# Two-layer hybrid trunk: output and second feed-forward products with tokens on partitions

## The chip, the cores and the metric

The kernel runs on one core of one Trainium2 chip. The metric is the device time of one execution in microseconds (us). Three executions of the kernel before took 1070.94, 1072.71 and 1075.98 us; the median is 1072.71 us.

## The reference

The program computes two layers of a trunk on 256 tokens of width 1024, in float32. Only the ends of the two halves of a layer matter here:

```
for l in range(2):
    u = rms_norm(x, pre_mix_norm_w[l])
    proj = u @ w_in[l]
    ...                                  # gated delta rule, latent attention, gates
    h = gates[:, :, 0] * y_a + gates[:, :, 1] * y_b
    x = x + rms_norm(h @ w_out[l], post_mix_norm_w[l])      # "out", 1024 x 1024
    u = rms_norm(x, pre_ffn_norm_w[l])
    f = square(relu(u @ w_ff1[l])) @ w_ff2[l]               # "ff1" 1024 x 4096, "ff2" 4096 x 1024
    x = x + rms_norm(f, post_ffn_norm_w[l])
```

`rms_norm(y, w)` is `y * rsqrt(mean(y*y over the 1024 features) + 1e-6) * w`.

## The kernel before

All activations lie with features on partitions: `xT` is 128 partitions x 8 chunks of features x 256 tokens. A float32 product is made of three fp32r products: the operand and the weight are each split into a high part (rounded) and a low part (the rest), and high x high, high x low and low x high are added up in PSUM.

The weights stream in pieces of 128x1024 float32 (512 KB), 152 a layer, through a ring of four places: SyncE issues the DMA into `raw`, ScalarE rounds it into `whi` (L973), VectorE subtracts into `wlo` (L1296), TensorE uses it in 24 matmuls (L559 to L561, in `chunk_products`) and raises `steps_done`, which frees the place. TensorE waits for `lo_ready`, which VectorE raises after each `wlo`.

The work is a list of jobs (`jobs_of_a_layer`), each with its pieces, and `schedule` writes one order, `ORDER`, that every engine walks through, doing its own part of each entry. Between the entries ScalarE and VectorE do the weight splits; `splits_wanted` (L488) says up to which piece each has to have split before its part of an entry, normally four pieces past the job's last one. So the place of a split in an engine's queue is fixed by the order in the program.

A job of "out" or "ff2" makes 256 features of all 256 tokens in one PSUM bank of `dense`: per 128x128 block of weights (stationary) three matmuls of 128x256 (the activations move). There are four such jobs of 2 pieces ("out") and four of 8 pieces ("ff2") a layer. After each, ScalarE squares the bank (L1095), VectorE multiplies it with the norm's weight into `yT` (L1591), and GpSimd adds up squares (L1697). After the fourth, `ysum` (L948) sums squares over features on TensorE by matmuls with a matrix of ones (L955), which leaves the row sum on every partition; ScalarE makes the inverse root by a logarithm and an exponential (L984, L986); VectorE multiplies `yT` with it and adds it to `xT` in pairs of chunks, two of the four adds done by GpSimd (`post`, L1612 and L1729). Then ScalarE rounds `xT` times the next norm's weight (`fuh` at L1037, or `xh` at L1003 for the next layer), VectorE takes the rest (`ful` at L1632, `xl` at L1303), and the next product starts, chunk by chunk: its first piece covers chunks 0 to 3, the second chunks 4 to 7. "ff1" comes after "out", the latent projection "lat" of the next layer after "ff2", the output DMAs after the last "ff2".

Of the kernel before, what the change touches and what calls it, by code (L numbers as in the profile page):

```python
# [19 lines left out]
ALU = mybir.AluOpType  # L20
# [3 lines left out]
P = 128  # L24
# [36 lines left out]
def jobs_of_a_layer():  # L61
# [3 lines left out]
    for kind, numbers, pieces in (("lat", range(3), 2), ("k", range(1), 2), ("z", range(1), 2), ("k", range(1, 4), 2),  # L65
# [4 lines left out]
                                  ("out", range(4), 2), ("ff1", range(16), 2), ("ff2", range(4), 8)):  # L70
# [8 lines left out]
EVAC_BY_ACT = {"v", "q", "k", "uq", "kn", "vt", "z", "gate"}  # L79
NJOB = len(JOBS)  # L80
NACT_EVAC = sum(k in EVAC_BY_ACT for k, _, _ in JOBS)
NDVE_EVAC = NJOB - NACT_EVAC
# [17 lines left out]
def evacs_through(j):  # L100

    mine = JOBS[j][0] in EVAC_BY_ACT
    return mine, sum((k in EVAC_BY_ACT) == mine for k, _, _ in JOBS[:j + 1])


def schedule():
# [129 lines left out]
    for i in range(4):  # L236
        job("ff2", i)
        if i in (1, 2):
            o.append(("yadd", 1 + i))
    o += [("ysum", 1), ("post", 1)]  # L240
# [7 lines left out]
def build(nc, x_in, pos_in, w_in, prm_in, cst_in, out):  # L248
    with ExitStack() as ctx:
# [32 lines left out]
        rs = keep("rs", [P, 4])  # L282
        bias_cols = keep("bias_cols", [P, 3])
# [68 lines left out]
        yT = ph("yT", [P, KD, S], 120)  # L352
# [47 lines left out]

        def S_(name):
            return ctx.enter_context(nc.semaphore(name))
# [18 lines left out]
        x_by_pool, x_by_dve, y_add = (signal("x_by_pool", 4), signal("x_by_dve", 4), signal("y_add", 4))  # L421
# [32 lines left out]
        h_hi, h_lo, y_sq, y_mm = (signal("h_hi", 4), signal("h_lo", 4), signal("y_sq", 8), signal("y_mm", 2))  # L454
        y_r, y_scaled, f_sq = (signal("y_r", 4), signal("y_scaled", 8), signal("f_sq", 16))
# [4 lines left out]
        def due(l, s, n):  # L460

            return l * rises_per_layer[s.name] + n

# [46 lines left out]
        def _(sp):  # L510
# [10 lines left out]
            for c in range(4):  # L521
                pair = slice(2 * c, 2 * c + 2)
                x_pair = x_by_pool if c % 2 else x_by_dve
                sp.wait_ge(x_pair, due(DEPTH, x_pair, 1 + c // 2))
# [5 lines left out]
        def _(pe):  # L530
# [3 lines left out]
            def banks_free(l, j):  # L534

                if j >= 3:
                    by_act, n = evacs_through(j - 3)
# [26 lines left out]
            def half(l, j):  # L564
# [7 lines left out]
                chunk_products(dense[j % 3], n, 0, 4, 256, uh, ul, True, False, KD, need).then_inc(steps_done, 1)  # L572

            def job(l, j):
                kind, i, pieces = JOBS[j]
                bank = dense[j % 3]
# [17 lines left out]
                elif kind in ("ya", "yb", "out"):  # L594
                    a_, b_ = {"ya": (oh, ol), "yb": (ah, al), "out": (hh, hl)}[kind]
# [3 lines left out]
                    def need(k):  # L599
                        if kind == "ya" and i == 0:  # L600
                            pe.wait_ge(on_lo, due(l, on_lo, k // 2 + 1))
                        if kind == "out" and i == 0:
                            pe.wait_ge(h_lo, due(l, h_lo, k // 2 + 1))
# [43 lines left out]
                elif kind == "ff2":  # L647
                    for h_, n in enumerate(pieces):
                        piece(l, n)
                        if i == 0:  # L650
                            pe.wait_ge(f_lo, due(l, f_lo, 2 * h_ + 2))
                        r = chunk_products(bank, n, 4 * h_, 4, 256, fh, fl, h_ == 0, h_ == 7, KF)
                        r.then_inc(steps_done, 1)
# [294 lines left out]
            def ysum(l, w):  # L948

                pe.wait_ge(y_add, due(l, y_add, 2 * w + 2))  # L950
                for n in range(2):
                    if n:
                        pe.wait_ge(y_sq, due(l, y_sq, 4 * w + 4))
                    for e in range(2):
                        r = mm(side[1][:, 0:S], ones, sq[n][:, e * S:(e + 1) * S], start=(n == 0 and e == 0),  # L955
                               stop=(n == 1 and e == 1))
                r.then_inc(y_mm, 1)
# [3 lines left out]
                      sc=sc, tr=tr, pv=pv, ysum=ysum, qrope=qrope)  # L961
# [7 lines left out]
        def _(act):  # L969
# [18 lines left out]
            def x_there(l, w, c):  # L988

                if l == 0 and w == 0:  # L990
                    act.wait_ge(s_x[c], 16)
                else:
                    x_pair = x_by_pool if c % 2 else x_by_dve
                    act.wait_ge(x_pair, due(l, x_pair, 1 + 2 * w + c // 2))

            def xsplit(l, part):

                for e in (range(2), range(2, KD))[part]:
                    if e % 2 == 0:
                        x_there(l, 0, e // 2)  # L1000
# [5 lines left out]
            def sq_(l, n):  # L1006
                w, c = divmod(n, 4)
                pair = slice(2 * c, 2 * c + 2)
                x_there(l, w, c)
# [21 lines left out]
            def fsplit_x(l, _):  # L1031

                for c in range(KD):
                    x_pair = x_by_pool if c // 2 % 2 else x_by_dve
                    if c % 2 == 0:
                        act.wait_ge(x_pair, due(l, x_pair, 3 + c // 4))
# [17 lines left out]
            def job(l, j):  # L1054
                kind, i, _ = JOBS[j]
                bank = dense[j % 3]
                if kind not in EVAC_BY_ACT and kind not in ("lat", "out", "ff2"):
                    return
                act.wait_ge(steps_done, products_done(l, j))
# [31 lines left out]
                elif kind in ("out", "ff2"):  # L1091
# [790 lines left out]
```

## Time and profile before

| | |
|---|---|
| median of three executions | 1072.71 us |
| span of the profiled execution, first to last instruction | 1064.2 us |
| TensorE busy (matmul) | 1010.9 us, 95% |
| VectorE busy | 732.4 us, 69% |
| ScalarE busy | 557.7 us, 52% |
| GpSimd busy | 137.9 us, 13% |
| mean granted TensorE clock | 0.985 |

The profiled execution has no time of its own beside its span. The span runs from the first to the last instruction; the median of the executions is 8.5 us above it. In the views, a time is the start in us from the span's start, and PEclk is the share of the full clock (2.4 GHz) that TensorE was granted, so 0.50 is 1.2 GHz.

### The profile page before, as it was taken

Reading aid. Unit: us, or ns where it says so; the run is one execution under the profiler, and the core shown is the slowest. Engines: PE = TensorE matmul, PEld = TensorE weight load, DVE = VectorE, ACT = ScalarE, POOL = GpSimd, SP = SyncE. Lnnn points to the kernel's source line nnn. Section 1 sums busy time; section 2 is a strip of 40 time slices with the busy share of each in tenths; the row PEclk is TensorE's granted clock in tenths of the full one; section 3 lists DMA queues with packets and bytes.
Section 4 is the critical chain, followed back from the end, with each engine's and each line's share of the span. In section 5 each row is a group of like instructions: output and inputs, shape, how many; then the busy total and the mean of one; then the engine's idle time right before and its main releaser. Section 6 shows DMA issues by size and latency. Waiting matters only on the chain.

```text
span 1064.2 us, 24113 instructions
## 1 busy us (share of the span) xinstructions
PE 1010.9 (95%) x10552; PEld 987.3 (93%) x10552; DVE 732.4 (69%) x982; ACT 557.7 (52%) x786; POOL 137.9 (13%) x109
## 2 busy tenths in 40 slices
PE   5899899999999899999978999999999989999996
PEld 5899889899999899999978998998999979999995
DVE  6886648698566698745388766677875777886453
ACT  6576365755444554443356753767454445444441
POOL 6201000230000322200010000014000013221001
PEclk9999999999999899999989999999999999999998
DMA  7344424334556176666534443334356544766661
GB/s 252 135 141 158 124 82 130 118 106 149 188 180 197 65 224 192 200 196 195 160 119 135 143 142 121 115 106 121 117 166 189 166 153 145 213 197 199 193 185 40
DMA packets 45608, 163.85 MB, mean 154 GB/s; under 512 B 5184, under 2 KB 5440, under 8 KB 45504
## 3 DMA queue, kind: packets, MB, share of 16 engines
q1 hardware_dynamic: 44928, 161.50, 48.2%
q8 instruction: 83, 1.36, 0.5%
q10 hardware_dynamic: 576, 0.82, 0.2%
q14 instruction: 21, 0.17, 0.0%
HBM read 161.25 MB, written 1.05 MB: 153 GB/s over the span
## 4 chain that ended last, share of the span: by engine, by line
PE 91%; DVE 5%; issue 2%; ACT 2%; DMA 1%; POOL 0%; POOLq 0%; SPq 0%; ACTq 0%; DVEq 0%
PE dense L559 25%; PE dense L560 25%; PE dense L561 24%; DVE wlo L1296 1%; PE sides L945 1%; PE sides L799 1%; PE sides L919 1%; PE sides L920 1%; PE sides L791 1%; DVE utmp L1332 1%; PE sides L955 1%; PE sides L759 1%; PE sides L769 1%; PE sides L895 1%; PE sides L718 1%
## 5 line engine op out<-in xcount | busy, mean ns | idle before, releaser
L1296 DVE TENSOR_TENSOR wlo<-raw,whi 128x1024 fp32r<-128x1024 f32 (+1 forms) x304 | 397.9, 1318 | 195.8 <-ACT whi L973 195.5
L973 ACT ACTIVATE whi<-raw 128x1024 fp32r<-128x1024 f32 (+1 forms) x304 | 315.6, 1047 | 225.7 <-PE dense L561 222.0
L559 PE MATMUL dense<-uh,whi 128*128 128x256 f32 x768 | 223.3, 291 | 5.3 <-DVE wlo L1296 5.3
L560 PE MATMUL dense<-ul,whi 128*128 128x256 f32 x768 | 216.3, 282 | 2.6 <-issue 2.6
L561 PE MATMUL dense<-uh,wlo 128*128 128x256 f32 x768 | 216.3, 282 | 0.0
L559 PEld LDWEIGHTS dense<-uh,whi 128*128 128x128 f32 x768 | 147.2, 192 | 7.8 <-DVE wlo L1296 5.7
L559 PE MATMUL dense<-fuh,whi 128*128 128x256 f32 x512 | 144.3, 282 | 9.9 <-DVE ful L1632 9.6
L561 PEld LDWEIGHTS dense<-uh,wlo 128*128 128x128 f32 x768 | 147.2, 192 | 1.6 <-issue 1.6
L560 PEld LDWEIGHTS dense<-ul,whi 128*128 128x128 f32 x768 | 146.7, 191 | 1.5 <-issue 1.3
L560 PE MATMUL dense<-ful,whi 128*128 128x256 f32 x512 | 143.5, 280 | 0.0
L561 PE MATMUL dense<-fuh,wlo 128*128 128x256 f32 x512 | 143.5, 280 | 0.0
L559 PE MATMUL dense<-fh,whi 128*128 128x256 f32 x512 | 141.3, 276 | 0.0
L560 PE MATMUL dense<-fl,whi 128*128 128x256 f32 x512 | 141.3, 276 | 0.0
L561 PE MATMUL dense<-fh,wlo 128*128 128x256 f32 x512 | 141.3, 276 | 0.0
L559 PEld LDWEIGHTS dense<-fuh,whi 128*128 128x128 f32 x512 | 98.3, 192 | 11.1 <-issue 10.3
L560 PEld LDWEIGHTS dense<-ful,whi 128*128 128x128 f32 x512 | 98.2, 192 | 0.1
L561 PEld LDWEIGHTS dense<-fuh,wlo 128*128 128x128 f32 x512 | 98.1, 192 | 0.0
L560 PEld LDWEIGHTS dense<-fl,whi 128*128 128x128 f32 x512 | 96.1, 188 | 0.0
L559 PEld LDWEIGHTS dense<-fh,whi 128*128 128x128 f32 x512 | 96.1, 188 | 0.0
L561 PEld LDWEIGHTS dense<-fh,wlo 128*128 128x128 f32 x512 | 96.1, 188 | 0.0
L1727 POOL TENSOR_TENSOR fr<-fr 128x512 f32<-128x512 f32 x32 | 46.5, 1453 | 119.3 <-DVE fr L1604 119.3
L1697 POOL TENSOR_TENSOR sq<-sq,sq 128x512 f32<-128x512 f32 x8 | 10.4, 1296 | 353.0 <-ACT sq L1095 353.0
(289 smaller groups left out, 1923.2 us busy)
## 6 DMA issues: line engine op xcount, KB each, us to landing
raw<-weights SPq DMA_DIRECT2D x304, 512.0 KB, 3.7
xT<-x_t SPq DMA_DIRECT2D x4, 256.0 KB, 5.7
out_t<-xT SPq DMA_DIRECT2D x4, 256.0 KB, 2.3
cst<-consts ACTq DMA_DIRECT2D x1, 512.0 KB, 6.5
prm_all<-params ACTq DMA_DIRECT2D x1, 150.0 KB, 4.0
pos_i<-pos ACTq DMA_DIRECT2D x1, 128.0 KB, 5.5
cst<-consts ACTq DMA_DIRECT2D x1, 6.0 KB, 5.8
```

The lines of the kernel that those rows point to most:

```text
L559: mm(o_, h_[:, ws], ahi[:, k0 + k, :], start=is_first, stop=False, skip_group_check=True)
L560: mm(o_, h_[:, ws], alo[:, k0 + k, :], start=False, stop=False, skip_group_check=True)
L561: x_ = mm(o_, l_[:, ws], ahi[:, k0 + k, :], start=False, stop=is_last, skip_group_check=True)
L718: r = mm(side[KS_BANK[i // 2]][:, c:c + 1], k_squares[i][:, e * S + t * P:e * S + (t + 1) * P], ones[:, 0:1], start=True, stop=True)
L759: r = mm(side[KK_BANK[n]][:, e * P:(e + 1) * P], kT[:, h, ts_], kT[:, h, ts_], start=True, stop=True)
L769: r = mm(side[QK_BANK[n]][:, e * P:(e + 1) * P], kT[:, h, ts_], qT[:, h, ts_], start=True, stop=True)
L791: r = mm(side[e][rows, 16 * g:16 * (g + 1)], LT[rows, g, e, rows], evens(Xq[rows, e, g, :], SIZES[lv]), start=True, stop=True)
L799: r = mm(side[e][rows, 16 * g:16 * (g + 1)], XTq[rows, e, g, :], PBq[rows, e, g, 0:16], start=True, stop=True)
L895: mm(side[2 + i % 2][:], ones, sq[i % 2][:], start=True, stop=True).then_inc(on_mm, 1)
L973: return A(o_, i_, ACT.Copy)
L1296: TT(wlo[s][:, 0:w], raw[s][:, 0:w], f32(whi[s][:, 0:w]), ALU.subtract).then_inc(lo_ready, 1)
L1727: G(fr[i % 4][:], fr[i % 4][:], fr[i % 4][:], ALU.mult).then_inc(f_sq, 1)
```

## The change

- "out" and "ff2" are each two jobs of 512 features (4 and 16 pieces). The activations of 128 tokens are now the stationary operand and 512 columns of weights move, so a matmul is 128x512 and there are half as many. The result has tokens on partitions, in four banks of `side`: `y_bank(f, t)` for feature half f and token half t.
- In the second job of each, the last two pieces (`HELD`) are first used for tokens 0 to 127 (`y_mm` is raised), then for tokens 128 to 255 (`steps_done`, twice).
- The sum of squares is a row sum, made by ScalarE's accumulator while it squares (`y_square`): after the first job for half the features, whose mean VectorE prepares (`ysq`), after the second for the rest. The matmuls with ones, GpSimd's additions, `yT` and the products with the inverse root as 128x256 tiles go.
- The inverse root is a 128x1 column. ScalarE scales the rows of tokens 0 to 127 and half of those of tokens 128 to 255 into `yr`, VectorE the other half. TensorE turns `yr` back by 16 transposes of 128x128 (`post`).
- VectorE multiplies each turned chunk with the norm's weight and adds it to `xT` in one instruction, chunk by chunk, in turn with the low parts. GpSimd does nothing there.
- The splits of the third and fourth piece past "out" move behind `post` and `fsplit_x`, to a new entry `("ahead", 0)` of the order.
- TensorE waits, at the end of the first job of each, for its own products before it raises `y_mm`.

```diff
-                                  ("out", range(4), 2), ("ff1", range(16), 2), ("ff2", range(4), 8)):
+                                  ("out", range(2), 4), ("ff1", range(16), 2), ("ff2", range(2), 16)):
...
-    for i in range(4):
-        job("out", i)
-        if i in (1, 2):
-            o.append(("yadd", i - 1))
-    o += [("ysum", 0), ("post", 0), ("fsplit_x", 0)]
+    job("out", 0)
+    o.append(("ysq", 0))
+    job("out", 1)
+    o += [("post", 0), ("fsplit_x", 0), ("ahead", 0)]
...
+        def turn_bank(w, c):
+
+            return [side[4], dense[2 if w else (BANK[JOB["ff1", 0]] + 2) % 3], side[0], side[2]][c]
...
             if what == "job":
-                ahead = 2 if n == NJOB - 1 else RING
+                ahead = RING - HELD if JOBS[n][:2] in (("out", 1), ("ff2", 1)) else RING
                 return min(l * NPIECE + JOBS[n][2][-1] + ahead, DEPTH * NPIECE)
...
+            if what == "ahead":
+                return l * NPIECE + JOBS[JOB["out", 1]][2][-1] + RING
...
+            def by_token(l, kind, f, pieces):
+
+                w = kind == "ff2"
+                a_, b_, low_ready = (fh, fl, f_lo) if w else (hh, hl, h_lo)
+
+                def token_products(p, n, t):
+                    bank = y_bank(f, t)
+                    for e in range(2):
+                        k = 2 * p + e
+                        ws = slice(e * 512, (e + 1) * 512)
+                        ts_ = slice(t * P, (t + 1) * P)
+                        last = k == 2 * len(pieces) - 1
+                        mm(bank[:], a_[:, k, ts_], whi[n % RING][:, ws], start=(k == 0), stop=False)
+                        mm(bank[:], a_[:, k, ts_], wlo[n % RING][:, ws], start=False, stop=False)
+                        r = mm(bank[:], b_[:, k, ts_], whi[n % RING][:, ws], start=False, stop=last)
+                    return r
+
+                held = HELD if f else 0
+                for p, n in enumerate(pieces[:len(pieces) - held]):
+                    piece(l, n)
+                    if f == 0:
+                        pe.wait_ge(low_ready, due(l, low_ready, p + 1))
+                    token_products(p, n, 0)
+                    r = token_products(p, n, 1)
+                    r.then_inc(steps_done, 1)
+                if f == 0:
+                    pe.wait_ge(steps_done, l * NSTEP + steps_through(JOB[kind, 0], job=True) + RING)
+                    pe.sem_inc(y_mm, 1)
+                    return
+                late = list(enumerate(pieces))[len(pieces) - held:]
+                for p, n in late:
+                    piece(l, n)
+                    r = token_products(p, n, 0)
+                r.then_inc(y_mm, 1)
+                for p, n in late:
+                    r = token_products(p, n, 1)
+                    r.then_inc(steps_done, 1)
...
             def post(l, w):
-                act.wait_ge(y_mm, due(l, y_mm, w + 1))
-                rsqrt(l, y_r, w, rn[0][:, 0:S], side[1][:, 0:S], 1.0 / D, 0.0)
+
+                def scaled(t, a_, b_):
+                    f = a_ // 512
+                    A(yr[:, t, a_:b_], y_bank(f, t)[:, a_ - 512 * f:b_ - 512 * f], ACT.Identity,
+                      scale=yss[:, 4 + t:5 + t]).then_inc(y_by_act, 1)
...
+                def add(e):
+                    dve.wait_ge(y_turned, due(l, y_turned, 4 * w + e // 2 + 1))
+                    STT(xT[:, e, :], turn_bank(w, e // 2)[:, e % 2 * S:(e % 2 + 1) * S], col(l, (POST_FFN if w else POST_MIX) + e),
+                        xT[:, e, :], ALU.mult, ALU.add).then_inc(x_new, 1)
...
+                dve.wait_ge(y_r, due(l, y_r, 4 * w + 4))
+                for c in range(2):
+                    part = slice(256 * c, 256 * (c + 1))
+                    TS(yr[:, 1, part], y_bank(0, 1)[:, part], yss[:, 5:6], None, ALU.mult).then_inc(y_by_dve, 1)
                 add(0)
-                times_norm(1)
-                low(0)
-                times_norm(2)
-                add(2)
-                low(1)
-                times_norm(3)
-                low(2)
-                low(3)
+                for e in range(KD):
+                    if e + 1 < KD:
+                        add(e + 1)
+                    low(e)
```

ScalarE between "out" and "ff1", in the kernel before: `sq` is the square of the last job's bank, `rn_68` the inverse root, `whi` a weight split.

```order
L973 ACTIVATE whi_55<-raw_51 128x1024 [waits steps_done,loaded1]
L973 ACTIVATE whi_56<-raw_52 128x1024 [waits steps_done,loaded2]
L1095 ACTIVATE sq_67<-dense 128x512 [waits y_add,steps_done]
L984 ACTIVATE rn_68<-sides,bias_cols 128x256 [waits y_mm]
L986 ACTIVATE rn_68<-rn_68 128x256 [waits y_r]
L1037 ACTIVATE fuh<-xT,prm_all 128x256 [waits x_by_dve]
```

And in the changed kernel, from the first square of the last job to the first splits of "ff1" (`yss` are columns of sums and roots).

```order
L1144 ACTIVATE sq_66,yss<-sides 128x512 [waits y_mm]
L1038 ACTIVATE yss<-yss 128x1 [waits y_mean,y_ss]
L1040 ACTIVATE yss<-yss 128x1 [waits y_r]
L1312 ACTIVATE yr<-sides,yss 128x512 [waits y_r]
L1312 ACTIVATE yr<-sides,yss 128x512
L1144 ACTIVATE sq_67,yss<-sides 128x512 [waits steps_done]
L1038 ACTIVATE yss<-yss 128x1 [waits y_mean,y_ss]
L1040 ACTIVATE yss<-yss 128x1 [waits y_r]
L1312 ACTIVATE yr<-sides,yss 128x256 [waits y_r]
L1312 ACTIVATE yr<-sides,yss 128x256
L1087 ACTIVATE fuh<-xT,prm_all 128x256 [waits x_new] x8
L1027 ACTIVATE whi_55<-raw_51 128x1024 [waits steps_done,loaded1]
```

The rounding of the second piece of "ff1" into `whi_55` stood ahead of the last square and now stands behind all eight `fuh`.

VectorE in the same place, in the kernel before, from the last weight splits of "out".

```order
L1296 TENSOR_TENSOR wlo_59<-raw_51,whi_55 128x1024 [waits hi_ready]
L1296 TENSOR_TENSOR wlo_60<-raw_52,whi_56 128x1024 [waits hi_ready]
L1591 TENSOR_SCALAR yT<-dense,prm_all 128x256 [waits y_sq,steps_done]
L1591 TENSOR_SCALAR yT<-dense,prm_all 128x256
L1618 TENSOR_TENSOR yT<-yT,rn_68 128x512 [waits dve_evac,y_r]
L1623 TENSOR_TENSOR xT<-xT,yT 128x512 [waits y_scaled]
L1618 TENSOR_TENSOR yT<-yT,rn_68 128x512
L1632 SCALAR_TENSOR_TENSOR ful<-xT,prm_all,fuh 128x256 [waits fu_hi,x_by_dve]
```

And in the changed kernel; the middle chunks, alike but for the bank, are left out by the break between the two pieces.

```order
L1701 TENSOR_SCALAR yr<-sides,yss 128x256 [waits y_r]
L1701 TENSOR_SCALAR yr<-sides,yss 128x256
L1686 SCALAR_TENSOR_TENSOR xT<-sides,prm_all,xT 128x256 [waits y_turned] x2
L1693 SCALAR_TENSOR_TENSOR ful<-xT,prm_all,fuh 128x256 [waits fu_hi]
L1686 SCALAR_TENSOR_TENSOR xT<-dense,prm_all,xT 128x256 [waits y_turned]
```

```order
L1686 SCALAR_TENSOR_TENSOR xT<-sides,prm_all,xT 128x256 [waits y_turned]
L1693 SCALAR_TENSOR_TENSOR ful<-xT,prm_all,fuh 128x256 [waits fu_hi] x2
L1369 TENSOR_TENSOR wlo_59<-raw_51,whi_55 128x1024 [waits hi_ready]
L1369 TENSOR_TENSOR wlo_60<-raw_52,whi_56 128x1024 [waits hi_ready]
L1369 TENSOR_TENSOR wlo_61<-raw_53,whi_57 128x1024 [waits hi_ready]
```

The subtraction into `wlo_59`, for which TensorE waits before the second piece of "ff1", stood ahead of the norm and now stands behind the last `ful`.

## Rows read from the trace of the kernel before

**Rows 1.** The page's busy time, share of the span and instructions, by engine.
```profile
PE 1010.9 (95%) x10552; PEld 987.3 (93%) x10552; DVE 732.4 (69%) x982; ACT 557.7 (52%) x786; POOL 137.9 (13%) x109
```
**Rows 2.** The page's chain that ended last, shares of the span by engine.
```profile
PE 91%; DVE 5%; issue 2%; ACT 2%; DMA 1%; POOL 0%; POOLq 0%; SPq 0%; ACTq 0%; DVEq 0%
```
**Rows 3.** Timeline, "out" to "ff1", first layer: start, duration, engine, instruction [idle before].
```profile
343.40 0.60 ACT L1095 ACTIVATE sq<-dense 128x512 f32<-128x512 f32 x1 [1.71 <-PE dense L561]
344.11 0.88 DVE L1591 TENSOR_SCALAR yT<-dense,prm_all 128x256 f32<-128x256 f32 x2 [1.15 <-ACT sq L1095]
345.22 0.47 ACT L984 ACTIVATE rn<-sides,bias_cols 128x256 f32<-128x256 f32 x1 [1.22 <-PE sides L955]
347.63 0.91 ACT L1037 ACTIVATE fuh<-xT,prm_all 128x256 fp32r<-128x256 f32 x2 [1.48 <-DVE xT L1623]
349.96 0.55 PE L559 MATMUL dense<-fuh,whi 128*128 128x256 f32 x1 [4.78 <-DVE ful L1632]
355.31 1.99 ACT L973 ACTIVATE whi<-raw 128x1024 fp32r<-128x1024 f32 x2
356.38 1.23 DVE L1296 TENSOR_TENSOR wlo<-raw,whi 128x1024 fp32r<-128x1024 f32 x1 [0.40 <-ACT whi L973]
```
**Rows 4.** Stretches there: length, busy PE, PEld, DVE, ACT, POOL, then PEclk, DMA.
```profile
348.00:349.00 1.00, 0.00 (x0) 0.00 (x0) 0.94 (x2) 0.54 (x2) 0.73 (x1) 0.97 0.00 0
349.00:350.00 1.00, 0.04 (x1) 0.07 (x1) 1.00 (x2) 0.43 (x2) 0.54 (x1) 0.50 0.00 0
355.00:356.00 1.00, 1.00 (x7) 1.00 (x7) 0.88 (x2) 1.00 (x3) 0.00 (x0) 0.62 0.00 0
```
**Rows 5.** Timeline of TensorE from "out" to "ff1" in the second layer.
```profile
867.46 1.98 PE L955 MATMUL sides<-sq,cst 128*128 128x256 f32 x8
874.22 0.36 PE L559 MATMUL dense<-fuh,whi 128*128 128x256 f32 x1 [4.78 <-DVE ful L1632]
```
**Rows 6.** Stretches of the second layer's start of "ff1", columns as in rows 4.
```profile
874.00:875.00 1.00, 0.78 (x5) 0.81 (x6) 1.00 (x3) 0.73 (x2) 0.00 (x0) 0.79 0.00 0
...
878.00:879.00 1.00, 1.00 (x11) 1.00 (x11) 1.00 (x1) 0.25 (x1) 0.72 (x1) 1.00 0.00 0
```
**Rows 7.** Timeline from "ff2" of the first layer to "lat" of the second.
```profile
529.59 0.60 ACT L1095 ACTIVATE sq<-dense 128x512 f32<-128x512 f32 x1 [7.04 <-PE dense L561]
537.51 0.87 DVE L1303 SCALAR_TENSOR_TENSOR xl<-xT,prm_all,xh 128x256 fp32r<-128x256 f32 x2
538.90 1.90 DVE L1303 SCALAR_TENSOR_TENSOR xl<-xT,prm_all,xh 128x256 fp32r<-128x256 f32 x2
543.17 0.38 PE L559 MATMUL dense<-xh,whi 128*128 128x256 f32 x1 [2.54 <-DVE wlo L1296]
547.82 0.60 ACT L1073 ACTIVATE sq_kv<-dense 128x512 f32<-128x512 f32 x1 [1.44 <-PE dense L561]
```
**Rows 8.** Timeline of the end of the program.
```profile
1052.46 0.60 ACT L1095 ACTIVATE sq<-dense 128x512 f32<-128x512 f32 x1 [9.76 <-PE dense L561]
1060.20 1.26 POOL L1733 TENSOR_TENSOR xT<-xT,yT 128x512 f32<-128x512 f32 x1 [1.23 <-DVE yT L1618]
```
**Rows 9.** Stretches of TensorE alone: length, busy (matmuls), PEclk, DMA share, GB/s.
```profile
276.00:336.00 60.00, 60.00 (x511) 1.00 0.58 184
370.00:430.00 60.00, 60.00 (x532) 1.00 0.68 210
940.00:1050.00 110.00, 110.00 (x973) 1.00 0.57 172
```
**Rows 10.** Timeline of TensorE in the "vt" job: start, duration, instruction.
```profile
193.71 0.39 PE L636 MATMUL dense<-wlo,lath 128*128 128x512 f32 x1
...
196.01 0.39 PE L637 MATMUL dense<-whi,latl 128*128 128x512 f32 x1
```
**Rows 11.** Groups of instructions: shapes, count, busy us, mean ns, idle before.
```profile
L1029 ACT ACTIVATE sm<-prm_all 128x8 f32<-128x8 f32 x2 | 0.4, 192 | 0.0
L931 PE MATMUL sides<-cst,E 128*128 128x128 f32 x48 | 7.2, 273 | 0.0
```

More of the change, by code:

```diff
@@ L79 @@
 EVAC_BY_ACT = {"v", "q", "k", "uq", "kn", "vt", "z", "gate"}
+BY_TOKEN = {"out", "ff2"}
+HELD = 2
 NJOB = len(JOBS)
 NACT_EVAC = sum(k in EVAC_BY_ACT for k, _, _ in JOBS)
-NDVE_EVAC = NJOB - NACT_EVAC
+NDVE_EVAC = sum(k not in EVAC_BY_ACT and k not in BY_TOKEN for k, _, _ in JOBS)
+BY_FEATURE = [j for j, (k, _, _) in enumerate(JOBS) if k not in BY_TOKEN]
+BANK = {j: n % 3 for n, j in enumerate(BY_FEATURE)}
 def steps_through(n, job=False):
@@ L102, in evacs_through @@
     mine = JOBS[j][0] in EVAC_BY_ACT
-    return mine, sum((k in EVAC_BY_ACT) == mine for k, _, _ in JOBS[:j + 1])
+    return mine, sum((k in EVAC_BY_ACT) == mine for k, _, _ in JOBS[:j + 1] if k not in BY_TOKEN)
 def schedule():
@@ L235, in schedule @@
     flush()
[L236 to L240, printed above, removed]
+    job("ff2", 0)
+    o.append(("ysq", 1))
+    job("ff2", 1)
+    o.append(("post", 1))
     return o
@@ L282, in build @@
         rs = keep("rs", [P, 4])
+        yss = keep("yss", [P, 8])
         bias_cols = keep("bias_cols", [P, 3])
@@ L1055, in job @@
                 kind, i, _ = JOBS[j]
-                bank = dense[j % 3]
-                if kind not in EVAC_BY_ACT and kind not in ("lat", "out", "ff2"):
+                if kind not in EVAC_BY_ACT and kind != "lat":
                     return
+                bank = dense[BANK[j]]
                 act.wait_ge(steps_done, products_done(l, j))
@@ L1090, in job, with y_square, ysq @@
                     copy(zs[:, pair, :], bank[:]).then_inc(act_evac, 1)
-                elif kind in ("out", "ff2"):
-                    w = kind == "ff2"
-                    if i >= 2:
-                        act.wait_ge(y_add, due(l, y_add, 2 * w + i - 1))
-                    A(sq[min(i, 1)][:], bank[:], ACT.Square).then_inc(y_sq, 1)
+            def y_square(l, w, f, t):
+                A(sq[t][:], y_bank(f, t)[:], ACT.Square, accum_out=yss[:, 2 * f + t:2 * f + t + 1]).then_inc(y_ss, 1)
+            def ysq(l, w):
+                act.wait_ge(y_mm, due(l, y_mm, 2 * w + 1))
+                for t in range(NT):
+                    y_square(l, w, 0, t)
             def silu(l, n):
@@ L1842, in lay_out_weights @@
                 pieces.append(np.pad(p_, ((0, 0), (0, PIECE - p_.shape[1]))))
-            elif kind == "ff2":
-                wide(w_ff2[lyr], 256 * i + r(256), KF)
+            elif kind in BY_TOKEN:
+                for p_ in range(KF // 2 if kind == "ff2" else KD // 2):
+                    pieces.append(blocks((w_ff2 if kind == "ff2" else w_out)[lyr], 2 * p_, 2, 512 * i + r(512)))
             else:
-                wide({"ya": w_a, "yb": w_b, "out": w_out, "ff1": w_ff1}[kind][lyr], 256 * i + r(256))
+                wide({"ya": w_a, "yb": w_b, "ff1": w_ff1}[kind][lyr], 256 * i + r(256))
     return np.ascontiguousarray(np.stack(pieces))
```

153 lines of the change are left out of this document (69 added, 84 removed).

## The prediction

> **What bounds the kernel now.** I read the busy shares first: TensorE is busy for 95% of the span, no other engine for more than 69% [rows 1]. The chain of waits agrees: 91% of what ended last is TensorE's own work [rows 2]. So a part of this change counts only if it alters how long TensorE works in "out" and "ff2", or how long it stands still, or runs at the low clock, at the four places where a norm over all features cuts the stream: "out" to "ff1" in each layer, "ff2" to "lat" between the layers, and the end. I read these in the timeline, with the granted clock beside it, and measure each from E, the start of ScalarE's square behind the last product.
>
> At the first "out" to "ff1", E is 343.40 and "ff1" starts at 349.96, 6.56 us later [rows 3]. The clock fell to 1.2 GHz at about 348.9 (0.97 in one stretch, 0.50 in the next), 3.7 us after the last matmul with ones (the logarithm that waits for it starts at 345.22), and rose within 355 to 356: a mean of 0.62 puts it at 355.76 [rows 4]. In the second layer "ff1" starts at 874.22, with E at 867.65 (the matmuls with ones start at 867.46, and E is 0.19 behind these, as at 343.21 and 343.40), again 6.57 us; the clock falls at about 874.6 (a mean of 0.79) and is low up to 878.0 [rows 5, 6]. Between the layers the second piece of "lat" starts 13.6 us after E, held by a weight split, and its job ends at about 547.5, 17.9 us after E [rows 7]. At the end the last addition is over at 1061.46, 9.0 us after E at 1052.46, and the span ends 2.7 us later [rows 8].
>
> **The streams.** Before, "out" has 192 and "ff2" 768 matmuls of 128x256 a layer. They stand 60/511 = 117.4 ns apart in the long stretch before "ff1" and 110/973 = 113.1 ns apart in "ff2" [rows 9]; the clock is 1.00 in both, so this kernel has two spacings at full clock. That makes 22.5 + 86.9 = 109.4 us a layer. After, there are 480 matmuls of 128x512. The trace has the very same triple in the "vt" job (activations stationary, then high, low and high weights moving): ten starts in 2.30 us, 230 ns [rows 10]. 480 x 0.230 = 110.4 us: 1.0 us more a layer, +2.1 in all. Halving the number of instructions gives nothing, because a matmul twice as wide takes 2.03 times 113.1 ns. The bounds: twice 113.1 ns would be 226.2 (-1.6 in all), twice 117.4 ns would be 234.8 (+6.6).
>
> **TensorE's wait for itself.** At the end of the first job of "out" and "ff2" it waits until its last matmul is over (0.39 us from its start instead of the 0.23 until the next could start [rows 10]), then loads weights and goes on. No row shows such a wait. With about 0.05 us for the signal and 0.11 for the first load I take 0.33 us each, four times: +1.3. Bounds: 0 (if the drain is hidden) and 0.6 each.
>
> **From the last product to the next.** With E = 0 at the square of tokens 128 to 255 (those of tokens 0 to 127 were squared and scaled while TensorE did their last 12 matmuls, 2.8 us, and their eight transposes run right after the products):
> - square 0.60 [rows 3], logarithm and exponential of one column at 0.19 each, by the nearest row, 128x8 [rows 11], with hand-overs: root at 1.1. Before it was there at 2.75, since the ones matmuls and two 128x256 functions of 0.47 and less came between.
> - VectorE scales 256 columns: 0.88 for two [rows 3], so the first is done at 1.6. Two transposes, 0.27 to the end of one and about 0.11 more for the second [rows 11]: turned at 2.2. Addition 0.45: 2.65. `fuh` 0.5 [rows 3]: 3.2. `ful` 0.45: 3.7. **TensorE starts at 3.75**, 2.8 us earlier than before.
> - Then VectorE does an addition and a low part per chunk, 0.80 us together (0.87 for two with the first one's latency [rows 7]; GpSimd no longer works beside it, where the pair took 1.90). TensorE at full clock needs 6 x 0.117 = 0.70 per chunk, so its first piece is over at about 6.9.
> - The second piece waits. VectorE's last low part ends at 9.1; the last `fuh` ends at 8.55, ScalarE's deferred split takes 1.04 (1.99 for two [rows 3]) until 9.6, VectorE's 1.23 until 10.9. **TensorE starts again at 10.95.** Before, this piece was split ahead of the norm, and the two behind it, made at 355.31 to 358 [rows 3], hindered nobody.
> - TensorE stands still for 4.0 us. The clock fell 3.7 us after TensorE had stopped in the one case, within 5.2 in the other (869.4 to 874.6) [rows 4, 5, 6], so it falls shortly before or after it starts again, and stays low for 3.4 us (874.6 to 878.0) to 6.8 us (348.9 to 355.76). Time at half the clock costs half of itself where TensorE works: 1.7 us for the short one; I take 2.0.
>
> The 48 matmuls of the first "ff1" job are then over at 10.95 + 24 x 0.117 + 2.0 = 15.75. Before, in layer 0: from 349.96 to 355.76 at 213 ns 27 matmuls, and 21 x 0.117 = 2.5: 358.2, or 14.8 after E. In layer 1: 19 matmuls up to 878.0, 29 x 0.113 = 3.3: 881.3, or 13.65. **So this place costs +0.95 and +2.1**, although the next product starts 2.8 us earlier. Bounds for each: -2 (no low clock) and +3.
>
> **Between the layers.** The same chain ends in `xh` and `xl`; one split is ahead, the second piece of "lat" was late before too. VectorE's eight low parts end at about 9.7 (ScalarE's split of that piece stands between the second and third `xh`, 1.04 us, but no longer behind GpSimd), its split at 10.9. The second piece runs 10.95 to 13.75, plus 2.0 for the clock: 15.75 against 17.9. **-2.2**, bounds -4.2 and -1.
>
> **The end.** Additions alone, 0.40 each, from 2.2: the last at 5.4 against 9.0, -3.6. The four output transfers now follow each other within 2.4 us, so I let them give back 0.5: **-3.1**, bounds -3.7 and -2.
>
> **The sum.** 2.1 + 1.3 + 0.95 + 2.1 - 2.2 - 3.1 = +1.2 us. From the profiled 1064.2 us span that is 1065.4; the median lies 8.5 us above the span, so 1072.7 becomes about 1074. What the four squares, eight `yT` products and GpSimd's sums of a norm cost before is nothing: they lay beside TensorE's stream, which no row shows waiting there; their removal counts nothing either.
>
> **A rule of the Trainium skill that bears on the streams.** Rows 9 and 10 give 113.1 and 230 ns. TensorE: Matmul & The Clock Gate, section "Back-to-back issue gap", has a warm gap of N/2.4 plus 2.5 ns, an estimate of 216 ns for 512 columns and 109 for 256. The 230 ns disagree with it by 14 ns. By it 480 x 0.216 = 103.7 us a layer, an estimate of 11 us less in both layers, and a time of about 1060. The trace decides, for the triple is the same; but "vt" is only 6 to 12 matmuls long.
>
> **Rivals.**
> 1. *The fixed part is halved.* What a 256-wide matmul takes beyond 256 columns at 2.4 GHz (113.1 - 106.7 = 6.4 ns) is paid once per 512 in a long, steady stream: 219.7 ns, 105.5 us a layer, -7.8 instead of +2.1, so 1064. For it: "vt" runs in short groups between other matmuls. Against: its spacing is 230 in the middle of a group too. Chance 0.08. By that rule of the Trainium skill it would go on to the estimate of 1060.
> 2. *The clock stays up.* If 4.0 us of standing still is too little for it to fall, the three places lose 2.0 less each: -6 us, 1068. For it: the transposes keep TensorE going to about 3. Against: it fell after 3.7 us. Chance 0.10.
> 3. *The slower spacing takes over.* There are two spacings at the same clock [rows 9], and the stretches change between them where the stream is interrupted; "ff1" and "ff2" now run at the fast one. If after the new interruptions the streams sit in the slow one: 480 x 2 x (234.8 - 230) ns = +4.6, and some 670 matmuls of "ff1" a layer at 4.3 ns more = +5.8. Together 1084, either alone about 1079. Decisive is whether "ff1" behind its norm is at 113 or 117 ns. For it: "ya", "yb" and "out" run slow through. Against: "ff1" went to the fast one in both layers. Chance 0.16.
> 4. *The change doesn't do what it says*: tokens 0 to 127 bring nothing, since their transposes wait behind the products in TensorE's queue and the chain starts with tokens 128 to 255 in any case. This is in my sum already; the chance lies with the forecast.
>
> **How the numbers follow.** Forecast (the streams even, starts earlier, second piece late): 0.66, own range 1069 to 1079. Within 0.5% is 5.4 us either way, about what a measurement can tell from no change: 1067.3 to 1078.1. Faster takes rival 1, half of rival 2 and 0.03 of the forecast: 0.16. Slower takes nearly all of rival 3 and 0.05 of the forecast: 0.20. Same: 0.64. The range of 8 in 10 goes from 1066 to 1081.
>
> **What would show it.** In the profile after: the spacing of the 128x512 matmuls in "ff2" (230 ns; 220 is rival 1, 235 rival 3); "ff1" starting 3.7 us after E; TensorE then waiting about 4 us for `wlo` before its second piece, twice, and once more in "lat"; the granted clock low behind each of these waits; a gap of 0.3 us after each first job; the last addition 5.4 us after E. I am wrong if the wait for `wlo` is absent or under 2 us, if the clock never falls there, or if a row sum costs ScalarE much more than a plain square, which no row shows.

## The result, and the profile after

Over 20 executions of each, the changed kernel has a median of 1083.12 us (1069.57 to 1087.73) and the kernel before 1071.34 us. The ratio is 1.0101, with a 95% interval of 1.0072 to 1.0130: about 11 us slower, and the median is outside the range of 1066 to 1081 us that was given. The ratios here and below leave out the executions more than 1.5% above the fastest of their kernel, among them one of e6 that took 1685 us at a mean granted clock of 0.56, so a ratio isn't the quotient of the two medians. The first profile of the changed kernel belongs to the fastest of its 20 executions, 1069.57 us with a span of 1067.8; so each execution takes 1.8 us more than its span, and a second profile, taken with the experiments, shows the common case.

The page of the first one: the shares of the engines, and those of the chain. Answers to [rows 1, 2].

```profile
PE 1020.4 (96%) x9624; PEld 951.8 (89%) x9624; DVE 710.4 (67%) x970; ACT 569.8 (53%) x826; POOL 117.0 (11%) x93
...
PE 90%; DVE 5%; ACT 2%; issue 2%; DMA 1%; SPq 0%; ACTq 0%; DVEq 0%
```

With 928 instructions fewer TensorE is busy 9.5 us longer. The timeline from "out" to "ff1" in the first layer of this kernel (start, duration, engine, instruction, idle before) answers to [rows 3]:

```profile
341.92 0.60 ACT L1144 ACTIVATE sq<-sides 128x512 f32<-128x512 f32 x1 [0.25 <-PE sides L680]
342.41 0.19 ACT L1144 ACTIVATION_READ_ACCUMULATOR sq<-sides 128x1 f32 x1
342.64 0.29 ACT L1038 ACTIVATE yss<-yss 128x1 f32<-128x1 f32 x1
343.20 0.87 DVE L1701 TENSOR_SCALAR yr<-sides,yss 128x256 f32<-128x256 f32 x2 [7.30 <-ACT yss L1040]
...
345.91 0.47 PE L577 MATMUL dense<-fuh,whi 128*128 128x256 f32 x1 [0.90 <-DVE ful L1693]
...
350.55 3.88 ACT L1027 ACTIVATE whi<-raw 128x1024 fp32r<-128x1024 f32 x4
351.62 4.63 DVE L1369 TENSOR_TENSOR wlo<-raw,whi 128x1024 fp32r<-128x1024 f32 x4 [0.46 <-ACT whi L1027]
...
352.90 0.58 PE L577 MATMUL dense<-fuh,whi 128*128 128x256 f32 x1 [2.40 <-DVE wlo L1369]
```

E is 341.92; "ff1" starts at E + 3.99 (before: 6.56) and its second piece at E + 10.98, released by the weight split that now stands behind the norm. The end of the program answers to [rows 8]; SPq is SyncE issuing the output:

```profile
1061.83 0.87 DVE L1686 SCALAR_TENSOR_TENSOR xT<-sides,prm_all,xT 128x256 f32<-128x256 f32 x2
1062.73 2.68 SPq L542 DMA_DIRECT2D out_t<-xT  x4
1063.41 1.65 DVE L1686 SCALAR_TENSOR_TENSOR xT<-sides,prm_all,xT 128x256 f32<-128x256 f32 x4
```

The last addition ends at 1065.06, 5.5 us after E, which is 1059.53 there (9.0 before), and the span ends 2.7 us later.

### The profile page after: what moved, and what is told of

It reads as the page before. It is cut to its first block, busy times and chain, and to the rows that moved or that the text cites. A ratio compares the mean times of both kernels' runs of the same rounds, so it can differ in the third digit from the quotient of the medians.

```text
span 1067.8 us, 22251 instructions
## 1 busy us (share of the span) xinstructions
PE 1020.4 (96%) x9624; PEld 951.8 (89%) x9624; DVE 710.4 (67%) x970; ACT 569.8 (53%) x826; POOL 117.0 (11%) x93
## 4 chain that ended last, share of the span: by engine, by line
PE 90%; DVE 5%; ACT 2%; issue 2%; DMA 1%; SPq 0%; ACTq 0%; DVEq 0%
PE dense L577 18%; PE dense L578 18%; PE dense L579 18%; PE sides L678 7%; PE sides L680 7%; PE sides L679 7%; DVE wlo L1369 1%; PE sides L994 1%; PE sides L969 1%; PE sides L968 1%; PE sides L848 1%; PE sides L840 1%; DVE xT L1686 1%; DVE utmp L1405 1%; ACT whi L1027 1%
## 5 line engine op out<-in xcount | busy, mean ns | idle before, releaser
L678 PE MATMUL sides<-whi,fh 128*128 128x512 f32 x256 | 101.4, 396 | 0.3
L680 PE MATMUL sides<-whi,fl 128*128 128x512 f32 x256 | 101.2, 395 | 0.0
L679 PE MATMUL sides<-wlo,fh 128*128 128x512 f32 x256 | 101.2, 395 | 0.0
L678 PEld LDWEIGHTS sides<-whi,fh 128*128 128x128 f32 x256 | 48.1, 188 | 12.5 <-DVE wlo L1369 1.1
L680 PEld LDWEIGHTS sides<-whi,fl 128*128 128x128 f32 x256 | 48.1, 188 | 11.6
L679 PEld LDWEIGHTS sides<-wlo,fh 128*128 128x128 f32 x256 | 48.1, 188 | 11.5
L577 PE MATMUL dense<-xh,whi 128*128 128x256 f32 x96 | 28.6, 298 | 15.7 <-DVE wlo L1369 14.8
```

The lines of the kernel that those rows point to most:

```text
L577: mm(o_, h_[:, ws], ahi[:, k0 + k, :], start=is_first, stop=False, skip_group_check=True)
L678: mm(bank[:], a_[:, k, ts_], whi[n % RING][:, ws], start=(k == 0), stop=False)
L679: mm(bank[:], a_[:, k, ts_], wlo[n % RING][:, ws], start=False, stop=False)
L680: r = mm(bank[:], b_[:, k, ts_], whi[n % RING][:, ws], start=False, stop=last)
```

## The experiments

Every ratio is to the kernel before, in runs on the same chip: e1 to e4 ran on one, e5 to e8 on a second, e9 to e12 on a third. Differences of ratios across these groups are less sure than those within one. The changed kernel itself has two ratios, 1.0101 from 20 executions and 1.0167 from 5 (e2), with medians 1 us apart; where a run is compared with it, both are given. "Fast spacings" are the 128x256 matmuls on weights of one profile whose successor starts less than 115.5 ns later, counted in the starts that the trace holds; nearly all others at full clock stand 117.8 ns apart (in e11 they are another pair, 115 and 120). There are some 6840 such pairs at full clock in a kernel with the old products, some 4970 in one with the new (those of "out" and "ff2" left out, in e4 and e8 too).

| run | ratio (95% interval) | median, us | fast spacings |
|---|---|---|---|
| before, first profile | | 1071.34 | 4256 |
| after, first profile | 1.0101 (1.0072 to 1.0130) | 1083.12 | 1495 |
| e1 before again | 1.0005 (0.9974 to 1.0036) | 1068.63 | 4177 |
| e2 after again | 1.0167 (1.0131 to 1.0203) | 1084.12 | 175 |
| e3 third piece ahead | 1.0015 (0.9987 to 1.0042) | 1068.04 | 174 |
| e4 moving 256 | 1.0086 (1.0050 to 1.0121) | 1077.66 | 228 |
| e5 before, tiles + 128 bytes | 1.0123 (1.0083 to 1.0163) | 1083.10 | 134 |
| e6 after, tiles at the old place | 1.0021 (0.9993 to 1.0049) | 1072.20 | 1931 |
| e7 = e3 and e6 | 0.9911 (0.9876 to 0.9946) | 1060.20 | 2138 |
| e8 = e7 and e4 | 0.9921 (0.9895 to 0.9948) | 1061.31 | 2680 |
| e9 before, tiles + 256 bytes | 0.9990 (0.9962 to 1.0018) | 1070.06 | 2869 |
| e10 before, everything + 128 bytes | 0.9998 (0.9967 to 1.0029) | 1071.20 | 2845 |
| e11 before, tiles - 64 bytes | 1.0209 (1.0181 to 1.0237) | 1094.07 | 737 |
| e12 tokens together | 0.9993 (0.9964 to 1.0023) | 1071.02 | 2856 |

### e1 and e2: both kernels again

No edit.

> The kernel before, unchanged, for a second profile of it. The profile before had a span of 1064.2 us, near the fastest of its executions, with 34.7 us at the low clock and 4256 of 6843 matmuls of 128x256 at the 113 ns spacing. If the share of slow spacing (117.8 ns) is a matter of chance per execution, it differs here, by up to 4.5 ns x 6800 = 30 us; if it is set by the program, it is the same within some tens of matmuls. Ratio 1.00.

> The changed kernel, unchanged, for a second profile. Theory A (streams): the 128x512 matmuls stand 233 ns apart again, which is 2.6 us more a layer than the 256-wide ones at 117.4 and 113.1, and the rest of the 11 us comes from the 256-wide stages sitting at 117.8 ns more often and from the clock. Theory B (the late piece): the wait for the second piece of ff1 (2.4 us) and a low clock behind it explain the rest. By A the profile shows more slow spacings than before's, by B more time at the low clock near 350 and 880. Ratio 1.007 to 1.013.

TensorE alone in "ff1" and "ff2" of e1, then of e2 (length, busy (matmuls), PEclk, DMA share, GB/s):

```profile
380.00:440.00 60.00, 60.00 (x532) 1.00 0.64 206
450.00:510.00 60.00, 60.00 (x532) 1.00 0.64 201
```

```profile
380.00:440.00 60.00, 60.00 (x512) 1.00 0.65 201
450.00:510.00 60.00, 59.85 (x258) 1.00 0.59 187
```

At the same clock of 1.00, "ff1" has 532 matmuls in 60 us before and 512 after, though nothing in "ff1" was changed: 113 and 117 ns. In "ff2" 258 of twice the width are 233 ns, a little over the 230 of "vt" [rows 10]. The slow spacing is not confined to the neighbourhood of the change. The last of the four "k" jobs, near the start and ahead of every changed instruction, has only fast spacings in both profiles of the kernel before and only slow ones in both of the changed kernel; here it is in e1, then in e2, 47 and 45 matmuls in 5 us:

```profile
63.60:68.60 5.00, 5.00 (x47) 1.00 0.57 156
```

```profile
64.80:69.80 5.00, 5.00 (x45) 1.00 0.56 179
```

The two profiles of the kernel before have nearly the same number of fast spacings, 4256 and 4177, but not quite in the same places: "lat" of the first layer has them for the most part in the first and hardly at all in e1. So the program sets the most of it, and not all. From E, the second piece of "ff1" starts in both profiles of the changed kernel and in both layers at 10.98. The clock of e2 behind that wait, which begins at 353.6 (length, busy PE, PEld, DVE, ACT, POOL, PEclk, DMA share, GB/s):

```profile
353.00:357.00 4.00, 0.57 (x5) 0.36 (x4) 3.35 (x7) 3.44 (x6) 0.00 (x0) 1.00 0.00 0
357.00:358.00 1.00, 0.69 (x5) 0.69 (x6) 1.00 (x2) 1.00 (x2) 0.00 (x0) 0.96 0.00 0
358.00:361.00 3.00, 3.00 (x16) 3.00 (x15) 2.67 (x3) 2.92 (x5) 1.04 (x1) 0.50 0.81 266
```

The clock falls to 1.2 GHz just after TensorE has gone on again (in the first profile, just before). So both theories have something in the profile, and two causes had to be told apart.

### e3: the third piece split ahead of the norm

```diff
-                ahead = RING - HELD if JOBS[n][:2] in (("out", 1), ("ff2", 1)) else RING
+                ahead = RING - HELD + 1 if JOBS[n][:2] in (("out", 1), ("ff2", 1)) else RING
```

> The third piece (second of ff1 and of lat) is split ahead of the norm, as before the change. Theory B: the waits for the low part of the weights (2.4 us and the like) go at three places, and with them a stretch of low clock each: 6 to 10 us less than the changed kernel, ratio to before 1.000 to 1.005. Theory A: TensorE is then bound by the low parts of the activations at 0.8 us a chunk, 2 to 3 us less at most for each place, 3 to 5 us in all; ratio 1.005 to 1.008.

The ratio falls from 1.0167 to 1.0015, about 16 us, more than either theory gave; against the 1.0101 of the 20 executions it is 9 us, as theory B had it. What TensorE waits for in the first layer, from 346.9 to 360 (engine, line, waited for: us, times, longest):

```profile
PE dense L577 <- DVE ful L1693: 0.9, 1, 0.9
PE dense L577 <- DVE wlo L1369: 0.8, 1, 0.8
```

The long wait has become 0.8 us, for the next piece. The 49th matmul of the consumer starts at E + 15.44, 15.10 ("ff1") and 14.87 ("lat") in e2, and at 11.08, 11.24 and 11.25 here: 11.8 us in all. The spacing is as slow as in e2, so this gain has nothing to do with it. The spans of the two profiles differ by 13.0 us, of which 3.3 lie ahead of E in the first layer, where the edit changes nothing. What the ratio has beyond 11.8 us is not placed.

### e4: the same products 256 columns wide

```diff
-                        mm(bank[:], a_[:, k, ts_], whi[n % RING][:, ws], start=(k == 0), stop=False)
-                        ...
+                        for q in range(2):
+                            ws = slice(e * 512 + q * 256, e * 512 + (q + 1) * 256)
+                            o_ = bank[:, q * 256:(q + 1) * 256]
+                            mm(o_, a_[:, k, ts_], whi[n % RING][:, ws], start=f_, ...)
+                            ...
```

> The changed kernel with each 128x512 matmul of out and ff2 made as two of 128x256, the weights loaded for each (1920 instead of 960). Theory A with the width as cause: the streams go back to 113 or 117.8 ns per 256 columns, that is -2.6 us a layer in ff2 if they are at 113, nothing if at 117.8. If the order of operands (activations stationary) is the cause of the slower spacing, they stay at 117 whatever the width. Ratio to before 1.005 to 1.011.

"ff2" takes 87.35 us in the first layer and 89.03 in the second, against 89.75 in both of e2. The spacing changes from job to job: both jobs of the first layer and the first of the second have the fast one, the last job the slow one (e4; the first and the second job of the second layer):

```profile
982.00:1024.00 42.00, 42.00 (x373) 1.00 0.62 198
1027.00:1069.00 42.00, 42.00 (x359) 1.00 0.37 114
```

So the order of the operands isn't the cause of the slow spacing: 256-wide matmuls with weights moving can have the fast one. Against e2 the ratio fell by 0.8%, more than these 3.1 us; against 1.0101 by 0.15%, less than them. How the time followed is open.

### e5 and e6: 128 bytes

The changed kernel declares one tile more, `yss`, 32 bytes a partition, ahead of the phase tiles. Their start is rounded up to a multiple of 128 bytes, plus 64, and had no room left: it moved from 93504 to 93632. e5 is the kernel before with that tile declared and unused, e6 the changed kernel with the phase tiles back where they were (`yss` lies in the gap in front of them). In both, as in the changed kernel, the small tile `bias_cols` behind `yss` lies 32 bytes further on.

```diff
+        yss = keep("yss", [P, 8])                                # e5, in the kernel before
```

```diff
-        R0 = (base[0] + 127) // 128 * 128 + 64                   # e6, in the changed kernel
+        R0 = (base[0] - 32 + 127) // 128 * 128 + 64
```

> The kernel before with the 32 unused bytes a partition of yss declared, and nothing else: the region of the phase tiles (activations, their low parts) then starts 128 bytes further on, at 93632 instead of 93504, as in the changed kernel. Theory C (address): TensorE's 256-wide matmuls fall to the 117.8 ns spacing nearly everywhere, as in all four profiles of changed kernels (175 to 1495 at 113 instead of 4200): 4000 x 4.5 ns = up to 18 us slower, ratio 1.010 to 1.017. Theory D (the new instructions set the spacing through the interruptions they make): no change, ratio 0.997 to 1.003.

> The changed kernel with its phase tiles back at the place that they have in the kernel before (yss lies in the gap in front). Theory C: over 2000 of its 256-wide matmuls go back to 113 ns, 9 to 12 us less than the changed kernel: ratio to before 1.000 to 1.006. Theory D: no change, ratio 1.010 to 1.016.

Declaring 32 unused bytes makes the kernel before 1.23% slower, and taking the shift back brings the changed kernel from 1.0101 (1.0167 in e2) to 1.0021, 0.8 or 1.5% faster. Its fast spacings go from 175 to 1931, a little under the 2000 expected. Theory C holds, D falls; that `bias_cols` moved is not the cause, since in e6 it lies where it does in the changed kernel. TensorE alone in e5, "ff1", "ff2" of the first layer and "ff2" of the second:

```profile
380.00:440.00 60.00, 60.00 (x511) 1.00 0.62 194
450.00:510.00 60.00, 60.00 (x512) 1.00 0.62 196
1000.00:1045.00 45.00, 45.00 (x384) 1.00 0.58 187
```

All at 117 ns; 1000 to 1045 has 400 matmuls in e1, 113 ns. "ff2" takes 90.33 us in both layers of e5 and 86.93 in both of e1. The 4000 fast spacings lost are worth 4000 x 4.45 ns = 18 us; the ratio says 13, and the span of e5 is 15 us above that of e1. The same shift costs 1.0% where the third piece is ahead (e3 to e7, 1.0015 to 0.9911, on two chips).

### e7 and e8: both mended, and 256 columns wide

e7 has the edits of e3 and e6, e8 that of e4 too.

> The third piece split ahead of the norm, and the phase tiles at the old place. If both causes are real and independent: 9 to 12 us less than with the third piece ahead alone, ratio to before 0.988 to 0.993. Theory D: ratio 1.000 to 1.003, as with the third piece alone.

> As the run before, and the products of out and ff2 as 128x256 matmuls. In the run with 256 columns at the shifted place three quarters of the ff2 matmuls stood 113 ns apart, which is 226.6 instead of 233.3 ns per 512 columns. If they all do here: 384 x 6.7 ns = 2.6 us a layer less, ratio to before 0.983 to 0.989.

e7 is faster than both kernels, 0.89% faster than the one before; the medians are 11 us apart. From the timeline of TensorE in e7, with E at 341.63:

```profile
345.63 0.35 PE L577 MATMUL dense<-fuh,whi 128*128 128x256 f32 x1 [0.91 <-DVE ful L1693]
...
352.72 0.36 PE L577 MATMUL dense<-fuh,whi 128*128 128x256 f32 x1 [0.78 <-DVE wlo L1369]
```

The start is as early as in the changed kernel, and the longest wait behind it is 0.8 us. e6 to e7 (1.0021 to 0.9911) is the price of the late piece without the shift: 12 us. e8 brings nothing beyond e7, and its forecast of 0.983 to 0.989 is missed. Its "ff2" takes 89.02 us in both layers, and that of e7 88.92 and 88.07: in e8 the first job of "ff2" has the fast spacing throughout and the second the slow one, in both layers (here the first):

```profile
437.00:479.00 42.00, 42.00 (x373) 1.00 0.63 195
481.00:523.00 42.00, 42.00 (x359) 1.00 0.62 188
```

Matmuls of 128x512 have two spacings as well, and each job of "ff2" has one of them throughout: 228.9 ns in three of the four jobs of e6 and of e7, 233.3 in the fourth, and 233.3 in all four jobs of each profile at the shifted place (after, e2, e3).

### e9, e10 and e11: which 128 bytes

```diff
-        R0 = (base[0] + 127) // 128 * 128 + 64
+        R0 = (base[0] + 127) // 128 * 128 + 64 + 256             # e9
+        R0 = (base[0] + 127) // 128 * 128                        # e11
-        base = [((nc.sbuf_base + 31) // 32) * 32]
+        base = [((nc.sbuf_base + 31) // 32) * 32 + 128]          # e10
```

> The kernel before with its phase tiles 256 bytes further on (93760), nothing else. If the spacing hangs on the tiles' place within 256 bytes, all is as before: over 4000 matmuls at 113 ns, ratio 0.997 to 1.003. If any other place than the old one is bad, or further away is worse, it is as slow as 128 bytes further: ratio 1.010 to 1.016.

> The kernel before with all its tiles, the weight ring too, 128 bytes further on. The phase tiles are then where they were in the slow run, but their distance to the ring is the old one. If the distance between the two operands of a matmul decides: fast, ratio 0.997 to 1.003. If the place of the phase tiles itself decides: slow, 1.010 to 1.016.

> The kernel before with its phase tiles 64 bytes nearer (93440, a multiple of 128). If only odd multiples of 64 bytes matter, or the half of 256 bytes in which the tiles begin, the count of 113 ns spacings tells: the same 4200, fewer, or more. No forecast of the sign: ratio 0.99 to 1.016.

256 bytes further is as good as the old place in time (0.9990), with 2869 fast spacings where over 4000 were expected. In e10 the phase tiles stand at the place of e5, but the ring has moved with them, and the loss is gone: not the place counts but the distance between the phase tiles and what lies in front. The weight ring, the other operand of these matmuls, is the likely partner, but it isn't tested apart from the other tiles there. 64 bytes nearer is worst of all, at 1.0209 outside even the wide range given, with most of the long streams at 120 ns (503 matmuls in the row, e11). Of the 737 in the table 690 are 115 ns apart, so the 113 ns are nearly gone:

```profile
380.00:440.00 60.00, 60.00 (x503) 1.00 0.63 197
```

At the good distance the fast spacing is no certainty. e9 has the slow one in "ff2" of the first layer and the fast one in the second:

```profile
450.00:510.00 60.00, 60.00 (x512) 1.00 0.62 193
1000.00:1045.00 45.00, 45.00 (x399) 1.00 0.62 192
```

In e10 it is the other way about. That makes up the difference between their 2850 fast spacings and the 4200 of the two profiles without an edit; whether it is chance, one profile of each can't tell. At the bad distance the slow one is nearly certain where activations move 256 wide, as in e2 to e5. The first profile of the changed kernel, with "ff1" at 113 ns in both layers, is an exception. It is also the fastest of the 20 executions, but its 1320 more fast spacings than e2 are worth only 6 of the 13.5 us to the median. The other exception is e4: with the weights moving 256 wide, three of four "ff2" jobs are fast at the bad distance.

### e12: the tokens together

e7, with the last two pieces used for all 256 tokens at once.

```diff
-                held = HELD if f else 0
+                held = 0
...
-                late = list(enumerate(pieces))[len(pieces) - held:]
-                ...
+                pe.wait_ge(steps_done, l * NSTEP + steps_through(JOB[kind, f], job=True) + RING)
+                pe.sem_inc(y_mm, 1)
...
-                ahead = RING - HELD + 1 if JOBS[n][:2] in (("out", 1), ("ff2", 1)) else RING
+                ahead = 2 if n == NJOB - 1 else RING
```

> The fast version of the change (third piece ahead, tiles at the old place), but the last two pieces used for all 256 tokens together, and the sums, the scaling and the transposes only then. The chain behind the last product gets longer by the square, the two functions and the scaling of the first half of the tokens on ScalarE (0.6 + 0.3 + 0.3 + 1.2 us, of which one part lies beside VectorE): ff1 starts 6 to 6.5 us after the last product instead of 4.4. At four places 1.5 to 2 us each: 6 to 8 us slower than that version, ratio to before 0.996 to 0.999. If it isn't on the path: ratio 0.991.

The ratio is 0.9993 against 0.9911: 9 us (on two chips; the spans of the profiles differ by 6.5), a little over what was expected. From its timeline, whose last product starts at 341.97:

```profile
342.49 0.60 ACT L1134 ACTIVATE sq<-sides 128x512 f32<-128x512 f32 x1 [1.72 <-PEq L692]
...
343.77 1.26 ACT L1302 ACTIVATE yr<-sides,yss 128x512 f32<-128x512 f32 x2
344.93 0.59 ACT L1134 ACTIVATE sq<-sides 128x512 f32<-128x512 f32 x1
...
349.16 0.36 PE L577 MATMUL dense<-fuh,whi 128*128 128x256 f32 x1 [0.79 <-DVE ful L1683]
```

"ff1" starts 7.19 us after the last product's start instead of 4.43: the square, functions and scaling of the first tokens, 342.49 to 344.93, are on the path. That is 2.76 us at each "out", and 2.6 us in front of "lat". The edit also took the early split in front of "lat" away, so that its second piece waits 3.3 us again (0.2 in e7). I had not meant that, and it is part of the 9 us. But that split doesn't touch the starts of "ff1", nor the last addition, which ends 2.5 us later after the last product than in e7, so serving half the tokens first is worth its place.

## Why the prediction was wrong, point by point

- **The start of the next product.** Forecast E + 3.75, measured 3.99 or 4.00 at each of the three places in the changed kernel, e2 to e4 and e6 to e8. Right. The row sum costs ScalarE 0.19 us more (the accumulator is read by an instruction of its own), the logarithm of one column 0.29.
- **The late piece.** Second piece at E + 10.95, measured 10.98; TensorE standing still 4.0 us, measured 4.02 in three of four cases (2.67 where the first piece ran at the low clock). The 49th matmul at 15.75, measured 15.4, 16.3, 15.4 and 15.1. Right, in cause, place and size. The costs of +0.95 and +2.1 against the kernel before came out as +0.5 and +2.5 in the first profiles and +0.7 twice between e1 and e2: the kernel before, too, has its 49th matmul at 14.9 and 13.7 in one profile and at 14.7 and 14.4 in the other, depending on how long the clock was low. Against a kernel with the short chain that splits the piece ahead, which the prediction did not weigh, the late piece costs 11.8 us in the profile and 9 to 16 in the ratios.
- **The clock.** It fell around each wait but one, as forecast: at E + 10.9, 9.4, 11.6, 12.4 and 10.2, and not at "lat" of the first profile. Rival 2 had it never falling. In all, the changed kernel is at the low clock for 24.1 and 22.9 us, the kernel before for 34.7 and 44.5 (e1), so the clock is no cause of the loss.
- **Between the layers.** The second piece at E + 10.60 for 10.95; its end 13.5 and 14.9 for 15.75, against 18.0 before: -4.5 and -3.2 for the -2.2 forecast, within its bounds.
- **TensorE's wait for itself.** 0.54 us from start to start instead of 0.23, and the next start comes 0.32 us later, so the wait costs 0.31 and 0.08, or 0.39 us, for the 0.33 forecast:

```profile
329.90 0.40 PE L680 MATMUL sides<-whi,hl 128*128 128x512 f32 x1
330.44 0.47 PE L678 MATMUL sides<-whi,hh 128*128 128x512 f32 x1
```

- **The end.** Last addition 5.5 us after E for 5.4. Right.
- **The streams.** 233 ns at the shifted place, where 230 was taken: "ff2" 89.75 us for 88.6 with its wait. At the old place (e6) it is 88.1 and 88.9. Rival 1, at 219.7 ns, falls, since no stream of this width in "ff2" is under 228.9. The rule of the Trainium skill (TensorE: Matmul & The Clock Gate, section "Back-to-back issue gap"), by which the estimate was 216 ns, is not borne out by any of the profiles. That section gives the rule for an isolated matmul, and for a stream with weight loads a figure of about 131 ns at 512 columns, which is further from the 228.9 and 233.3 measured.
- **The step that failed** is the one that the sum took for granted: that "ff1", "lat" and all the stages that the diff doesn't touch would keep their spacing, "the streams even". The prediction has no word on the diff's line `yss = keep("yss", [P, 8])`, so the sum holds nothing for it. It moved every phase tile by 128 bytes against the weight ring, and with that the spacings from a mixture of 113 and 117.8 ns to nearly all 117.8: about 4000 of them in the kernel before (e5), about 1750 in the changed kernel (e6 to e2). e5 shows this by itself (+1.23%), e6 that without it the change costs +0.21% (-0.07% to +0.49%), 2 us, where the sum said 1.2. The profiles of e1 and e2 add up to it: outside "out" and "ff2" 2470 fast spacings fewer are 11 us, "ff2" is 2 x 2.8 us longer, and the four places of the norms give back 5.2 us where the sum had 2.25. That is 11.4 of the 11.8 us between their spans.
- **Rival 3** named what happened, the slower spacing taking over, at a price of 10 us that is near the 11 measured. It had the wrong cause: it expected the interruptions of the stream to decide. With the same interruptions e6 has over ten times as many fast spacings as e2. That its size fits is in part luck: it priced "out", "ff2" and "ff1" alone, while some 1080 of the spacings lost, near 5 us, lie in other stages, and the norms gave back 3 us more than the sum had. The prediction saw two spacings at one clock and did not ask what sets them.
- **The base.** The 1072.7 us of three executions are 1071.3 in 20, which changes little. But the 8.5 us between the profiled span and the median are not time around the span, which is 1.8 us. The profiled execution was one of the faster ones.

What stays open: why the distance within 256 bytes sets the spacing, which pair of tiles matters, what tips a stage one way or the other at the good distance and, in e4, at the bad one, and a few microseconds of the ratios of e3 and e4.

## What to carry to other kernels

When a change adds a tile, compare the addresses of everything behind it, and if they have moved, time the old kernel with the tile declared and unused before anything is said of the change itself. When a norm's chain is made shorter, look at what the freed time runs into: a weight split that was harmless ahead of the chain became the longest wait when it was put behind it, and moving it back was worth more (12 us, e6 to e7) than the whole change in its best form (0.89%, e7). A single profile of a kernel whose executions scatter by 1.5% is one draw: read the effect in spacings and waits from two, and the time from many executions.

## What the runs showed of the hardware

- A stream of 128x256 fp32r matmuls with their weight loads has two steady spacings at the full clock of 2.4 GHz, 113.3 and 117.8 ns. It keeps one for up to 1400 matmuls ("ff1" and "ff2" of e5 and e9) and changes it only where the even stream is interrupted; others, 115 and 120 ns, appear with the operands 64 bytes off (e11). Streams of 128x512 have 228.9 and 233.3 ns, the second alone at the shifted place.
- The distance of the phase tiles from the tiles in front, the weight ring among them, decides how often the fast one occurs in the kernel before: 4256, 4177, 2869 and 2845 times at the old distance or 256 bytes more, 134 at 128 more, 47 at 64 less (without those of 115 ns).
- ScalarE's row sum adds an instruction that reads the accumulator, 0.19 us.
